# Gathering and turning a pair of expert blocks' token rows at once, in the expert stage of a hybrid encoder kernel

## What is computed

```
ht = rmsnorm(x, ffn_norm_g)                 # 512 rows of 2048
g_sel = argmax(ht @ rg_w + rg_b)            # one of 4 groups
top_v, top_i = top_k(expert logits of that group, 2)
gate = g_prob[g_sel] * softmax(top_v)
for each of 32 experts e, over the rows that chose it:
    y = (silu(xb @ w_gate[e]) * (xb @ w_up[e])) @ w_down[e]     # 2048 -> 512 -> 2048
    out[token] += gate * y
```

## Time and profile before

| what | value |
|---|---|
| median of 3 runs | 1858.61 us (1856.91 to 1858.63) |
| profiled execution | 1858.32 us, span 1856.6 us |
| tensor engine busy | 1655.0 us, 89% of the span |
| vector, scalar, gpsimd busy | 696.8, 335.9, 174.0 us |
| read from DRAM | 484.29 MB |
| expert blocks, from the first gather on | 828.8 us to the end |

### The profile page before, as it was taken

How to read it: one execution, slowest core, us unless ns; L and a number is a source line. 1 busy time by engine, 2 the same in 40 slices (tenths; PEclk the granted TensorE clock), 3 DMA queues, 4 the chain that set the end, 5 groups by cost and what they waited for, 6 DMA issues and landing times.

```text
span 1856.6 us, 20772 instructions
## 1 busy us (share of the span) xinstructions
PE 1655.0 (89%) x7715; PEld 929.8 (50%) x7715; DVE 696.8 (38%) x1014; ACT 335.9 (18%) x578; POOL 174.0 (9%) x255
## 2 busy tenths in 40 slices
PE   7979999989999959939989998998898899889997
PEld 6557788868887444733333333333233333333333
DVE  1467766554344241341322332233133223323333
ACT  3132243442221021401101010100101010011001
POOL 0182044320000000010000000000000000000000
PEclk9989999999999989959999999999999999999998
DMA  7213322244235110408999999999999999999994
GB/s 278 86 46 91 91 55 60 65 128 155 91 112 228 45 46 0 182 10 347 402 408 413 415 407 412 403 409 397 411 399 406 410 397 411 404 416 403 414 417 172
DMA packets 115096, 484.40 MB, mean 261 GB/s; under 512 B 9602, under 2 KB 47596, under 8 KB 62060
## 3 DMA queue, kind: packets, MB, share of 16 engines
q1 hardware_dynamic: 110864, 470.84, 64.8%
q0 software_dynamic: 3456, 12.88, 2.3%
q10 hardware_dynamic: 732, 0.07, 0.0%
HBM read 484.29 MB, written 8.39 MB: 265 GB/s over the span
## 4 chain that ended last, share of the span: by engine, by line
PE 66%; DMA 20%; DVE 9%; issue 2%; ACT 2%; SPq 0%; ACTq 0%; POOL 0%; DVEq 0%; POOLq 0%
DMA weight_ring<-in_expert_w_up_dram 20%; PE ps L1675 16%; PE ps L1385 10%; PE ps L1499 9%; PE ps L1702 6%; DVE residual L1268 4%; PE ps L1652 3%; PE ps L1582 3%; PE ps L1518 3%; PE ps L1330 2%; PE ps L1654 2%; PE ps L1345 2%; PE ps L1358 1%; PE ps L1591 1%; PE ps L1419 1%
## 5 line engine op out<-in xcount | busy, mean ns | idle before, releaser
L1675 PE MATMUL ps<-weight_ring,transposed_acts 128*64 128x512 f32 x2048 | 470.6, 597 | 59.4 <-DMA weight_ring<-in_expert_w_up_dram 58.6
L1675 PEld LDWEIGHTS ps<-weight_ring,transposed_acts 128*64 128x64 f32 x2048 | 157.3, 137 | 366.6 <-issue 252.1
L1702 PE MATMUL ps<-weight_ring,transposed_acts 128*64 128x512 f32 x1024 | 228.5, 599 | 18.2 <-issue 16.1
L1268 DVE TENSOR_TENSOR residual<-ps,residual 128x512 f32<-128x512 f32 x256 | 165.2, 687 | 24.0 <-PE ps L1654 24.0
L1288 DVE SCALAR_TENSOR_TENSOR y_low<-ps,proj_buffer,y_high 64x1024 fp32r<-64x1024 f32 x64 | 82.1, 1283 | 238.3 <-ACT y_high L832 237.3
L1652 PE MATMUL ps<-y_high,spread 128*128 128x512 f32 x256 | 127.3, 497 | 28.0 <-DVE residual L1268 23.9
L1702 PEld LDWEIGHTS ps<-weight_ring,transposed_acts 128*64 128x64 f32 x1024 | 72.3, 137 | 155.8 <-issue 153.2
L1258 DVE TENSOR_TENSOR transposed_acts<-ps,ffn_gain_by_row 128x512 f32<-128x512 f32 x66 | 42.5, 684 | 245.3 <-PE ps L1634 245.2
L832 ACT ACTIVATE y_high<-ps,proj_buffer 64x1024 fp32r<-64x1024 f32 x64 | 70.9, 1108 | 325.7 <-PE ps L1702 324.9
L1385 PE MATMUL ps<-mix_high,w_in_high 128*128 128x512 f32 x288 | 117.8, 409 | 9.3 <-DVE w_in_low L941 9.3
L1385 PE MATMUL ps<-normed_low,w_in_high 128*128 128x512 f32 x288 | 113.2, 393 | 0.0
(11 more groups left out here) (253 smaller groups left out, 1892.4 us busy)
## 6 DMA issues: line engine op xcount, KB each, us to landing
weight_ring<-in_expert_w_gate_dram SPq DMA_DIRECT2D x128, 1024.0 KB, 23.4
weight_ring<-in_expert_w_up_dram SPq DMA_DIRECT2D x128, 1024.0 KB, 25.3
weight_ring<-in_expert_w_down_dram SPq DMA_DIRECT2D x128, 1024.0 KB, 18.3
weight_ring<-in_w_in_dram SPq DMA_DIRECT2D x18, 1024.0 KB, 5.6
weight_ring<-in_w_out_dram SPq DMA_DIRECT2D x16, 1024.0 KB, 5.1
weight_ring<-in_xkv_w_dram SPq DMA_DIRECT2D x8, 1024.0 KB, 5.6
residual<-in_x_dram SPq DMA_DIRECT2D x8, 1024.0 KB, 18.7
weight_ring<-in_xq_w_dram SPq DMA_DIRECT2D x4, 1024.0 KB, 5.4
```

The source lines that it names most:

```text
L1268: v.tensor_tensor(X[:, t, n * 512:(n + 1) * 512], ps[:, 6 + i % 2, :], X[:, t, n * 512:(n + 1) * 512], ALU.add).then_inc(sum_ready if last ...
L1675: ins = mm(ps[side * SLOTS:(side + 1) * SLOTS, 0, :], xsT[:, par, k, :], w[:, kk, :], start=(k == 0), stop=(k == KD - 1), skip_group_check ...
L1702: ins = mm(ps[half, 4 + n // 2, :], act_t[:, f * SLOTS:(f + 1) * SLOTS], w[:, n * 512:(n + 1) * 512], start=(f == 0), stop=(f == KF - 1), ...
```

## The change

Rows are gathered once for a pair of blocks, 128 slots in 128 partitions, with one column of `tokf` as the list. The tensor engine transposes them with 16 transposes of 128 rows x 128 values into four PSUM banks (2, 3, 6 and 7), and the vector engine copies them out in four operations of 128 x 512. There is one buffer of rows and one `xsT` for a pair, in place of two halves each. The turning for the next pair stands in the odd block, between the gate and up products and the transposes L1688; the even block has none. The wait for the adding of the parts (`part_added`), which stood behind L1688 in the odd block, now stands ahead of the turning, since the turning writes banks 6 and 7. Block 0 waits for the turned rows of blocks 0 and 1, and its gather has 128 slots. On the vector engine the four copies stand in the odd block behind the product for `act_t`.

```diff
+TURN_BANKS = (2, 3, 6, 7)
-        cols = sb("slot_columns", [SLOTS, 2], I32)
+        cols = sb("slot_columns", [P, 1], I32)
-        xsT = Hf[:, 0:2 * KD * SLOTS].rearrange("p (b k n) -> p b k n", b=2, n=SLOTS)
+        xsT = Hf[:, 0:KD * P].rearrange("p (k n) -> p k n", n=P)
-        gathered = [sem("gathered0"), sem("gathered1")]
+        gathered = sem("gathered")
...
-            def step(b, par):
-                wait_past(pool, xs_turned, b * 2)
-                g.tensor_copy(cols[:, 1 - par:2 - par], tidx[:, ds(b + 1, 1)]).then_inc(idx_copied, 1)
...
-                g.indirect_dma_start(out=xs[0:SLOTS, 1 - par, :], out_offset=None, in_=hn_dram,
-                                     in_offset=bass.IndirectOffsetOnAxis(ap=cols[:, 1 - par:2 - par], axis=0),
-                                     bounds_check=S - 1, oob_is_err=False).then_inc(gathered[1 - par], 16)
+            def gather(pair):
+                column, copied, turned_ = pair * 2, pair + 1, pair * 4
...
+                wait_past(pool, xs_turned, turned_)
+                g.tensor_copy(cols[:, 0:1], tokf[:, ds(column, 1)]).then_inc(idx_copied, 1)
+                pool.wait_ge(table_ready, 1)
+                pool.wait_ge(idx_copied, copied)
+                g.indirect_dma_start(out=xs, out_offset=None, in_=hn_dram,
+                                     in_offset=bass.IndirectOffsetOnAxis(ap=cols[:, 0:1], axis=0),
+                                     bounds_check=S - 1, oob_is_err=False).then_inc(gathered, 16)
...
-            def turn_evac(b, par):
-                for q in range(2):
-                    dve.wait_ge(xs_turned, b * 2 + (q + 1))
-                    v.tensor_tensor(xsT[:, par, 8 * q:8 * q + 8, :],
-                                    ps[:, 2 + q, 0:8 * SLOTS].rearrange("p (k n) -> p k n", n=SLOTS),
+            def turn_evac(pair):
+                for q in range(4):
+                    dve.wait_ge(xs_turned, pair * 4 + (q + 1))
+                    v.tensor_tensor(xsT[:, 4 * q:4 * q + 4, :],
+                                    ps[:, TURN_BANKS[q], :].rearrange("p (k n) -> p k n", n=P),
...
                 if par == 0 and pair is not None:
-                    turn_evac(b + 1, 1 - par)
                     add_parts(pair * 16 - 16, 0)
...
                 if par == 0 and pair is not None:
                     add_parts(pair * 16 - 16, 1)
-                else:
-                    turn_evac(b + 1, 1 - par)
                 if par == 1:
+                    turn_evac(1 if pair is None else pair + 1)
...
+            def turn_rows(pair):
+                rows = pair * 16 + 16
...
+                pe.wait_ge(table_ready, 1)
+                pe.wait_ge(gathered, rows)
+                for q in range(4):
+                    for k in range(4 * q, 4 * q + 4):
+                        ins = turn(ps[:, TURN_BANKS[q], (k % 4) * P:(k % 4 + 1) * P],
+                                   hs[:, 0, k * P:(k + 1) * P], ident[:, :])
+                    ins.then_inc(xs_turned, 1)
...
             def block_pe(b, par, pair):
-                pe.wait_ge(xsT_ready, b * 2 + 2)
+                if par == 0:
+                    pe.wait_ge(xsT_ready, b * 2 + 4)
...
-                            ins = mm(ps[side * SLOTS:(side + 1) * SLOTS, 0, :], xsT[:, par, k, :], w[:, kk, :],
+                            ins = mm(ps[side * SLOTS:(side + 1) * SLOTS, 0, :], xsT[:, k, par * SLOTS:(par + 1) * SLOTS], w[:, kk, :],
...
-                turn_rows(b + 1, 1 - par)
+                if par == 1:
+                    if pair is not None:
+                        pe.wait_ge(part_added, pair * 16)
+                    turn_rows(1 if pair is None else pair + 1)
...
-                if par == 1 and pair is not None:
-                    pe.wait_ge(part_added, pair * 16)
```

More of the change, by code:

```diff
@@ L554, in _ @@
             pool.wait_ge(table_ready, 1)
-            xs = hs
-            def reg(value):
-                return value if isinstance(value, int) else pool.to_reg(value)
+            xs = hs[:, 0, :]
             g.iota(tramp, pattern=[[1, S]], base=0, channel_multiplier=0,
                    allow_small_or_imprecise_dtypes=True).then_inc(tramp_ready, 1)
[L562 to L566, removed]
@@ L568, in step @@
-            def step(b, par):
-                wait_past(pool, xs_turned, b * 2)
-                g.tensor_copy(cols[:, 1 - par:2 - par], tidx[:, ds(b + 1, 1)]).then_inc(idx_copied, 1)
-                copied = reg(b + 2)
+            def gather(pair):
+                column, copied, turned_ = pair * 2, pair + 1, pair * 4
+                if not isinstance(pair, int):
+                    copied, turned_ = pool.to_reg(copied), pool.to_reg(turned_)
+                wait_past(pool, xs_turned, turned_)
+                g.tensor_copy(cols[:, 0:1], tokf[:, ds(column, 1)]).then_inc(idx_copied, 1)
@@ L585, in _ @@
-            pool.wait_ge(gathered[0], 16 * (NE // 2 + 1))
+                g.indirect_dma_start(out=xs, out_offset=None, in_=hn_dram,
+                                     in_offset=bass.IndirectOffsetOnAxis(ap=cols[:, 0:1], axis=0),
+                                     bounds_check=S - 1, oob_is_err=False).then_inc(gathered, 16)
+            gather(0)
+            gather(1)
+            with pool.Fori(2, NE // 2 + 1) as it:
+                gather(it)
+            pool.wait_ge(gathered, 16 * (NE // 2 + 1))
@@ L586, in _ @@
             more = pool.value_load(meta[0:1, NOVER:NOVER + 1], min_val=0, max_val=NOVER)
             with pool.If(more > 0):
[L588 to L592, removed]
+                with pool.Fori(NE // 2 + 1, NBLK // 2 + 1) as it:
+                    gather(it)
+                pool.wait_ge(gathered, 16 * (NBLK // 2 + 1))
@@ L1294, in _ @@
             dve.wait_ge(tramp_ready, 1)
-            turn_evac(0, 0)
+            turn_evac(0)
             block_dve(0, 0, None)
@@ L1617, in _ @@
             ins.then_inc(table_done, 1)
[L1620 to L1635, removed]
+            def turn_rows(pair):
+                rows = pair * 16 + 16
+                if not isinstance(pair, int):
+                    rows = pe.to_reg(rows)
+                pe.wait_ge(table_ready, 1)
[4 more added lines that the diff above has]
+                                   hs[:, 0, k * P:(k + 1) * P], ident[:, :])
                     ins.then_inc(xs_turned, 1)
@@ L1704, in block_pe @@
                     ins.then_inc(used, 1)
-            turn_rows(0, 0)
+            turn_rows(0)
             block_pe(0, 0, None)
```

2 lines of the change are left out of this document (1 added, 1 removed).

## The result

The changed kernel takes 1824.45 us (median of 4 runs, 1824.35 to 1827.31) against 1857.76 us for the kernel before on the same chip: a ratio of 0.9826, 95% interval 0.9809 to 0.9843. It is 1.7% faster, 33 us, where the prediction saw 2 us. The profiled execution took 1824.49 us, with a span of 1822.3 us (1856.6 before).

The account below looks back on a forecast made before the run. The prediction took the never-pausing weight stream as the bound. Start +2.2, block 3 -1.9, gathers -1.8 and tail -0.5 make -2.0 us on 1858.32, 1856.3; the median, 0.3 above, 1856.6 us, range 1851 to 1866.

Parts of the forecast that it names:

- The row costs 2.3 times its bytes, and that price stays.: Weight stream: a gathered row costs 0.045 us, 2.3 times its bytes, and the change leaves that price alone.
- rival B: Weight stream: rows in gathers of 64 cost more than in 32; at 0.010 us each 1865.8 us; chance 0.13.
- The stream: gathers, -1.8 us.: Weight stream: 28 gathers become 14, each with 0.13 us of its own, 1.8 us less.
- Rival A: Weight stream: each gather has a larger price of its own, 0.34 us or more; 1853.7 or 1851.4 us; chance 0.14.
- The stream: block 3, -1.9 us.: Weight stream: block 3's rows are fetched ahead of the first used slot instead of within the stream, 1.9 us less.
- The start, +2.2 us.: Ahead of the weight stream: longer landing and turning delay the first load, +2.2 us, between +0.6 and +3.6.
- (b): At the start: 16 transposes of 128 columns instead of 64, at the lower clock, take 1.6 us more.
- (d): At the start: an estimate for the rise of the clock, 0.8 us taken off the sum.
- Within a pair, -0.5 us, hidden.: Engine work of a pair: even block 1.15 us less, odd block's turning 0.7 more; -0.5 us, hidden in the stream.
- The tail, -0.5 us.: Behind the last awaited load at 1786.4 us: the last pair's balance of engine work counts, -0.5 us.
- C: Weight stream: up to 9 us put on the fuller of a pair's two blocks; chance 0.04, half of it slower.
- D: Expert stage: the tensor engine is the bound after all and its 0.5 us a pair shows; 1849.6 us; chance 0.03.

Follow-up runs that it names:

- e7_stride2: Kernel before with each gather's list of 64 slots written to partitions 0, 2, ..., 126 instead of neighbouring ones: 1836.39 us, ratio 0.9885.
- e9_w32s4: Kernel before with lists of 32 slots, rows past a block's 32nd left out, written to partitions 0, 4, ..., 124: 1817.07 us, ratio 0.9783.
- e2_two128: Changed kernel with two gathers of 128 slots a pair, the other half's slots absent, odd blocks' rows left out of the result: 1829.84 us, ratio 0.9846.
- e3_before128: Kernel before, turning and all, with lists of 128 slots of which the upper 64 are absent: 1851.17 us, ratio 0.9961.
- e5_halves: Kernel before with lists of 128 slots, even blocks in the lower 64, odd in the upper 64, turning once a block: 1827.55 us, ratio 0.9838.
- e1_two64: Changed kernel with each pair's gather cut in two of 64 slots, to the lower and upper 64 partitions: 1865.53 us, ratio 1.0035.
- e10_even: Changed kernel with a block's tokens spread over its 64 slots, first eight to partitions 0, 4, ..., 28 of its half: 1819.54 us, ratio 0.979.
- e8_w32: Kernel before with lists of 32 slots to partitions 0 to 31, rows past a block's 32nd left out: 1843.74 us, ratio 0.9921.
- e4_far: Kernel before with rows read from the down weights, 256 KB apart, instead of the normed rows: 1858.57 us, ratio 1.0.
- e6_w96: Kernel before with lists of 96 slots, the upper 32 absent: 1890.78 us, ratio 1.0183.

## Why the prediction was wrong

**"The row costs 2.3 times its bytes, and that price stays."** This is the step that failed. The first half was measured rightly. The second was assumed: no row of before spoke for it, since all of before's gathers had the same shape. The price belonged to the lists of before, of 64 slots that land in neighbouring partitions (0.050 us). e7_stride2 and e9_w32s4 take it away by moving the rows and nothing else (0.021 and 0.019 us), e2_two128 and e3_before128 by a longer list to the same partitions (0.021 and 0.022 us). Gone in all blocks, with both halves in use, it is worth 29.8 us of stream (e5_halves) of the 31.8. The prediction did suspect that a row's price might depend on the width (rival B) and let it go one way only, dearer; neither the sum nor the range had a case in which it got cheaper. The price that a row has beside its bytes, 0.025 us x 922 rows = 23 us in the prediction's own numbers, was the largest in the stream, and the change altered the form of every transfer that paid it.

**The stream: gathers, -1.8 us.** The size is about right. e5_halves and the changed kernel differ by 2.0 us in the stream, block 3 included, and by 2.2 in the medians, with intervals that overlap; e2_two128, with twice the gathers of after, has a stream 1.2 us longer. Rival A is refuted: 14 gathers at 0.34 us would be 4.8.

**The stream: block 3, -1.9 us.** The mechanism is there: the queue's bytes after 844 us fell by 0.25 MB. At the price of a row now, its share is 0.6 us; at the old price the 1.95 us that were counted.

**The start, +2.2 us.** It measured +0.1. (a) Landing, predicted +1.4: +0.7. (b) Turning, +1.6: 1.97 to 3.51 us, +1.5. (c) Nothing, as predicted: the products begin 0.78 us behind the last turn in both. (d) The clock is the 0.8 that the sum takes off. No run shows that term; it was an estimate for a rise that comes as long after the first turn as before. What the runs showed in its place is 2.2 us: before, the clock was at 0.50 until about 839.7 us (0.71 is the mean of the window in which it rose), 7.1 us after the first turn, and in after it was at the full level from about 835.0 us, 3.3 us after the first turn. The products' 64 records then took 13.95 us instead of 16.11. The early rise repeats in the two other traces of the changed kernel, after_again and after_third, in the windows in which the clock rose:

```profile
835.00:838.00 3.00, 2.21 (x11) 1.34 (x11) 1.81 (x3) 0.00 (x0) 0.68 (x2) 0.79 0.00 0
```

```profile
836.00:839.00 3.00, 2.16 (x14) 1.35 (x14) 1.84 (x3) 0.00 (x0) 0.85 (x2) 0.87 0.00 0
```

The means put the rise at 836.3 and 836.8 us, 3.5 and 2.9 us after the first turn (832.75 and 833.89) and about a microsecond ahead of the first product (837.17 and 838.06). In these three traces the rise came when only transposes had run. What does set it stays open: e1_two64 has the same turns, and its clock rose only about 9.4 us after the first (833.63), well into the products.

**Within a pair, -0.5 us, hidden.** Right in its parts: from the landing to the next load it is 38.4 us before and 37.2 after (the even block's turning gone, 1.15 predicted), and the odd block's turning takes 1.90 instead of 1.15. The prediction had 1.83 for it by a slip: 32 products in 3.82 us are 0.119 us each and not 0.114, so that sixteen take 1.91. The tensor engine's wait for the up chunks was to grow to 60 us or more and fell to 39.0. That follows from the failed step: the stream's period fell by 1.6 us between the two pairs shown, and by 2.1 us on average (31.8 us over 15 pairs), more than the engine's work did, and the stream is still the bound.

**The tail, -0.5 us.** It measured -1.0. The last even block is 1.2 us shorter up to the turns (37.72 to 36.54 us in the chains) and the turns are 0.75 longer; the other -0.6 us lies behind them, and its cause stays open.

**The rivals.** B has its sign reversed: a row in the wide gather is cheaper. C, with a chance of 0.04 and half of it slower, put up to 9 us on the fuller of a pair's two blocks; that was an estimate, and no run shows which DMA engine carries a row. What the runs show is that the partitions of the rows matter beside their price: the stream is 23.9 us longer with all rows in the lower half (e3_before128) than in both halves in turn (e5_halves), and 5.6 us shorter with a block's rows spread (e10_even) than in after. In after, with both blocks of a pair in one list, the rate stayed at 421 GB/s at a DMA share of 1.01, with no loss of that kind to see. D is refuted by the 39.0 us of waits and by the even period of the loads.

## What was shown, what was inferred, what is open

Shown, as the price of one window each: with the list unchanged, other partitions took a row from 0.050 us to 0.021 (before, e7_stride2) and from 0.052 to 0.019 (e8_w32, e9_w32s4); with the partitions unchanged, a list of 128 took it from 0.050 to 0.022 (before, e3_before128) and from 0.057 to 0.021 (e1_two64, e2_two128). Twice the gathers left it at 0.021 (e2_two128), another source at 0.054 (e4_far), turning once for a pair at 0.057 (e1_two64) and turning once a block at 0.020 (e5_halves). Shown too: a second cost, of idle DMA engines. The DMA share fell to 0.71 and 0.52 in short stretches of e3_before128, to 0.94 in one of e7_stride2, and was 0.99 over the steady stretch of e6_w96. Not every list to part of the partitions has it: the share was 1.01 over 844 to 1740 us in before (64 partitions) and in e8_w32 (32).

Not shown: where the idle time comes from. The views show queues and not engines, so which engine writes which partitions can't be read from them. What the traces have is that e3_before128, with its rows in the lower half alone, has a stream 23.9 us longer than e5_halves with the same bytes, and that its rate holds at 421 GB/s until 1090 us before it falls to 405 to 410.

Open: what makes the row dear at the destination. Both strided lists also reach the upper 64 partitions, which before never writes, so that they don't separate a wider spacing from the use of both halves; a list of 32 in every second partition of the lower half would have done it. That the lower half isn't dear as such is shown by e3_before128 (0.022 us), and that the upper half isn't cheap as such by e1_two64 (0.057 us for rows in both).

## What to carry to other kernels

Where a stream of transfers is the bound, price every transfer in it against its bytes; one that costs more than them has a reason, and an estimate that holds the excess fixed while its shape changes assumes the answer. For a gather into on-chip memory beside a saturated stream, try a full-width list whose unused slots are absent, or a stride, so that the rows spread over all 128 partitions. It is worth 0.03 us for each row of 8 KB here (29.8 us of stream in e5_halves), more than halving the number of gathers and turns (2.0 us, e5_halves against after). Then look at how the used slots are spread over the partitions; spreading each block's rows took another 5.6 us off the stream (e10_even). What idle DMA engines looked like in e3_before128 is a DMA share of 0.98 to 0.99 in place of 1.01, with the rate down by 3% (405 to 410 GB/s of 421), and short stretches in which the share falls to 0.71 and 0.52.

## What the runs showed of the hardware, beyond what I expected

A row of 8 KB in a saturated stream takes 0.019 to 0.022 us with the lists over the full width or strided, and 0.05 to 0.057 with 32, 64 or 96 slots in neighbouring partitions. A list of 128 took gpsimd 1.09 us against 0.99 for 64, and the absent slots of e2_two128, with twice the gathers, cost at most 1.2 us of stream. The same turning at the same place was followed by the full clock after 2.9 to 3.5 us in three traces of the changed kernel, and after 9.4 us in e1_two64.
